# A weight half split inside attention one, banks released one by one, post norms reordered, half-tile stores

## The reference, cut to what matters

```
x = x + conformer_conv(rms_norm(x)); x = x + swiglu(rms_norm(x))       # first block, layer 0
q, k, v, f from rms_norm(x); o = forgetting_attention(q, k, v, f)      # "attention one", 16 heads
x = x + o @ w_o; x = x + moe(rms_norm(x)); x = rms_norm(x)             # layer 1, 8 experts
mix = concat(attention two, gated delta net) @ w_out_2                 # second block
x = x + rms_norm(mix) * post_mix_norm
m = relu(rms_norm(x) @ w_up_2)^2 @ w_down_2
x = x + rms_norm(m) * post_mlp_norm                                    # the output
```

## Time and profile before

| | before |
|---|---|
| time, median of 3 runs | 1800.59 us (1797.88 to 1801.01) |
| the profiled execution | 1803.72 us |
| its span, first to last instruction | 1801.9 us |
| PE busy (matmul) | 1703.9 us, 95% |
| DVE busy | 1272.4 us, 71% |
| ACT busy | 985.6 us, 55% |
| mean granted PE clock | 0.966 of full speed |
| bytes moved | 401.48 MB, mean 223 GB/s |

### The profile page before, as it was taken

One profiled execution on the slowest core, in us unless ns is written; L12 is line 12 of the kernel. 1 busy time (PEld: TensorE's weight loads), 2 busy tenths in 40 slices (PEclk: granted clock), 3 DMA queues, 4 the chain that ended last, 5 costly groups with the idle time before them and its releaser, 6 DMA issues.

```text
span 1801.9 us, 24579 instructions
## 1 busy us (share of the span) xinstructions
PE 1703.9 (95%) x9718; PEld 1493.2 (83%) x9718; DVE 1272.4 (71%) x1306; ACT 985.6 (55%) x1071; POOL 16.2 (1%) x22
## 2 busy tenths in 40 slices
PE   6988999898989999999999999999969999979998
PEld 5867999797878888888888888888859989969997
DVE  4964444545369898888888898988878477555554
ACT  3333444445357777777777776777755441344443
POOL 1000000000000000000000000000000000000000
PEclk9999999899969999999999999999989899989999
DMA  6404554533119898988989898989964300035550
GB/s 267 152 0 187 187 187 164 187 140 141 40 60 373 333 351 323 368 338 347 371 316 369 328 352 331 362 317 372 354 259 164 140 2 1 1 140 187 187 187 24
DMA packets 31189, 401.48 MB, mean 223 GB/s; under 512 B 3688, under 2 KB 3952, under 8 KB 5520
## 3 DMA queue, kind: packets, MB, share of 16 engines
q1 hardware_dynamic: 30704, 399.44, 58.6%
q0 software_dynamic: 416, 1.06, 0.2%
HBM read 399.43 MB, written 1.06 MB: 222 GB/s over the span
## 4 chain that ended last, share of the span: by engine, by line
PE 80%; DVE 8%; DMA 5%; ACT 4%; issue 3%; SPq 0%; DVEq 0%; ACTq 0%
PE ps L1845 21%; PE ps L1847 21%; PE ps L1846 21%; DMA raw<-in_ws 4%; PE ps L1903 3%; DVE wl L876 2%; PE ps L2351 2%; ACT wh L871 2%; PE ps L1919 2%; PE ps L2004 2%; PE ps L2339 1%; PE ps L2161 1%; DMA ring<-in_ws 1%; PE ps L2151 1%; DVE wl L762 1%
## 5 line engine op out<-in xcount | busy, mean ns | idle before, releaser
L876 DVE TENSOR_TENSOR wl<-raw,wh 128x2048 fp32r<-128x2048 f32 x266 | 607.8, 2290 | 90.7 <-ACT wh L871 87.7
L871 ACT ACTIVATE wh<-raw 128x2048 fp32r<-128x2048 f32 x264 | 506.4, 1919 | 200.7 <-PE ps L1847 82.3
L1845 PE MATMUL ps<-wh,f_r 128*128 128x512 f32 (+1 forms) x1200 | 461.3, 384 | 8.9 <-DVE wl L876 6.3
L1846 PE MATMUL ps<-wl,f_r 128*128 128x512 f32 (+1 forms) x1200 | 455.2, 379 | 0.0
L1847 PE MATMUL ps<-wh,f_r 128*128 128x512 f32 (+1 forms) x1136 | 430.3, 379 | 0.0
L1845 PEld LDWEIGHTS ps<-wh,f_r 128*128 128x128 f32 x1200 | 227.0, 189 | 53.7 <-DVE wl L876 9.2
L1846 PEld LDWEIGHTS ps<-wl,f_r 128*128 128x128 f32 x1200 | 227.2, 189 | 40.8
L1845 PE MATMUL ps<-ht_t_r,wh 128*128 128x256 f32 x832 | 241.0, 290 | 8.8 <-DVEq L655 6.6
L1847 PEld LDWEIGHTS ps<-wh,f_r 128*128 128x128 f32 x1136 | 214.3, 189 | 40.4
L1847 PE MATMUL ps<-ht_t_r,wl 128*128 128x256 f32 x832 | 239.8, 288 | 0.0
L1846 PE MATMUL ps<-h_t_r,wh 128*128 128x256 f32 x832 | 238.6, 287 | 0.0
(11 more groups left out here) (406 smaller groups left out, 2017.5 us busy)
## 6 DMA issues: line engine op xcount, KB each, us to landing
raw<-in_ws SPq DMA_DIRECT2D x169, 2048.0 KB, 9.0
raw<-in_ws SPq DMA_DIRECT2D x25, 1024.0 KB, 5.2
ring<-in_ws SPq DMA_DIRECT2D x6, 2048.0 KB, 11.2
gb<-in_gains SPq DMA_DIRECT2D x5, 512.0 KB, 8.5
x_t<-in_x SPq DMA_DIRECT2D x1, 1024.0 KB, 5.0
f<-scratch POOLq DMA_DIRECT2D x8, 128.0 KB, 3.0
out<-x_t SPq DMA_DIRECT2D x2, 512.0 KB, 2.6
cst<-in_const SPq DMA_DIRECT2D x1, 964.5 KB, 6.9
```

The costliest lines, as they stand in the source:

```text
L871: nc.scalar.activation(half_of(wh, h % SPLIT), raw_half(h % HALVES), ACT.Copy).then_inc(S("high"), 1)
L876: nc.vector.tensor_tensor(half_of(wl, h % SPLIT), raw_half(h % HALVES), half_of(wh, h % SPLIT).bitcast(F32), ALU.subtract).then_inc(S("spl ...
L1845: first = nc.tensor.matmul(bank, xh, h, start=start, stop=False)
L1846: nc.tensor.matmul(bank, xh, l, start=False, stop=False)
```

## The change

Four edits. (1) The split of half W2 leaves its place ahead of attention one. ACT makes its high part in two quarters of 1024 columns in steps 4 and 6, DVE the low part in two quarters in steps 8 and 10, each behind that step's exponentials or maxima. (2) DVE frees bank (T,u,j-1) after it has issued the low tiles of bank j (in norm 2: those of the first gain), and only the last one behind the loop. (3) In the post norms DVE adds eps to the first sum of squares in place and multiplies each bank with the norm weights before the root; ACT takes the root of one sum with the other as bias, without the separate addition; behind the root DVE does one multiply-add of M2, the inverse root and X ("mix": one of 1024 columns, "mlp": two of 512). (4) The output goes out in four stores of 256 KB in place of two of 512 KB.

```diff
--- before.py
+++ after.py
@@ -564,9 +564,11 @@
                     sp.wait_ge(S("gb1_used"), 1)
                     sp.dma_start(gb[:, D:2 * D], dr["gains"][3, :].partition_broadcast(P)).then_inc(S("ld_gb1"), 16)
             for tt in range(TT):
-                sp.wait_ge(S("y_ready"), tt + 1)
-                sp.dma_start(out[tt * P:(tt + 1) * P, :], X[:, tt, :]).then_inc(S("stored"), 16)
-            sp.wait_ge(S("stored"), 16 * TT)
+                for c in range(2):
+                    cols = slice(c * 512, (c + 1) * 512)
+                    sp.wait_ge(S("y_ready"), 2 * tt + c + 1)
+                    sp.dma_start(out[tt * P:(tt + 1) * P, cols], X[:, tt, cols]).then_inc(S("stored"), 16)
+            sp.wait_ge(S("stored"), 16 * 2 * TT)
 
 
         @block.gpsimd
@@ -650,9 +652,11 @@
                         src = bank[:, (c % 2) * SEQ:(c % 2 + 1) * SEQ].rearrange("p (t s) -> p t s", t=TT)
                         nc.vector.scalar_tensor_tensor(pair.lo[:, c], src, V(gname, c), pair.hi[:, c].bitcast(F32),
                                                        ALU.mult, ALU.subtract).then_inc(S("ht_lo"), 1)
+                    if j and gname == gains[0][0]:
+                        dve.wait_ge(S("ht_lo"), n - 2 * len(gains))
+                        dve.sem_inc(B.free[B.at[("T", u, j - 1)][0]], 1)
             dve.wait_ge(S("ht_lo"), n)
-            for j in range(4):
-                dve.sem_inc(B.free[B.at[("T", u, j)][0]], 1)
+            dve.sem_inc(B.free[B.at[("T", u, 3)][0]], 1)
 
         def root(dve, ch, tt, order):
 
@@ -725,21 +729,37 @@
                     ins.then_inc(S("q_ready"), 1)
             let_go(B, (name, n), ins)
 
-        def high_pre(act):
-
-            h = count("high_pre")
+        def quarter(a, part):
+            return a[:, part * HALF // 2:(part + 1) * HALF // 2]
+
+        def high_pre(act, quarter_of=None):
+
+            h = todo["high_pre"] if quarter_of == 0 else count("high_pre")
             n, part = pre_unit(h)
             k = (n - N_PRE) % RAW
             act.wait_ge(S(f"ld_w{k}"), 16 * sum(1 for m in range(n + 1) if (m - N_PRE) % RAW == k))
             if h >= SPLIT:
                 act.wait_ge(S("p_used"), h - SPLIT + 1)
-            nc.scalar.activation(half_of(wh, h % SPLIT), half_of(raw, 2 * k + part), ACT.Copy).then_inc(S("p_high"), 1)
-
-        def low_pre(dve):
-
-            h = count("low_pre")
+            if quarter_of is None:
+                nc.scalar.activation(half_of(wh, h % SPLIT), half_of(raw, 2 * k + part), ACT.Copy).then_inc(S("p_high"), 1)
+            else:
+                nc.scalar.activation(quarter(half_of(wh, h % SPLIT), quarter_of), quarter(half_of(raw, 2 * k + part), quarter_of),
+                                     ACT.Copy).then_inc(S("p_high" if quarter_of else "p_quarter"), 1)
+
+        def low_pre(dve, quarter_of=None):
+
+            h = todo["low_pre"] if quarter_of == 0 else count("low_pre")
             n, part = pre_unit(h)
-            dve.wait_ge(S("p_high"), h + 1)
+            if quarter_of == 0:
+                dve.wait_ge(S("p_quarter"), 1)
+            else:
+                dve.wait_ge(S("p_high"), h + 1)
+            if quarter_of is not None:
+                k = 2 * ((n - N_PRE) % RAW) + part
+                nc.vector.tensor_tensor(quarter(half_of(wl, h % SPLIT), quarter_of), quarter(half_of(raw, k), quarter_of),
+                                        quarter(half_of(wh, h % SPLIT), quarter_of).bitcast(F32),
+                                        ALU.subtract).then_inc(S("p_split" if quarter_of else "p_lower"), 1)
+                return
             nc.vector.tensor_tensor(half_of(wl, h % SPLIT), half_of(raw, 2 * ((n - N_PRE) % RAW) + part),
                                     half_of(wh, h % SPLIT).bitcast(F32), ALU.subtract).then_inc(S("p_split"), 1)
 
@@ -820,7 +840,7 @@
                 if s and todo["low_post"] < 2 * N_POST:
                     low_post(dve)
 
-        def attention_act(act, B, a, heads, base):
+        def attention_act(act, B, a, heads, base, beside={}):
 
             PR, PT = PRS[a], PTS[a]
             def heads_out(n):
@@ -845,6 +865,8 @@
                     ins = nc.scalar.activation(PR[:, h % 2, 256:384], bank[:, 256:384], ACT.Exp, bias=rt[:, 65 + m:66 + m],
                                                accum_out=SUMS[:, 0, h:h + 1])
                     let_go(B, ("S", a, h), ins)
+                if h in beside:
+                    beside[h]()
                 if a == 0 and h >= 8 and h % 4 == 0:
                     heads_out((h - 8) // 4)
             if a == 0:
@@ -914,12 +936,10 @@
                     at = tt * D + c * 512
                     nc.scalar.activation(ht_t[:, at:at + 512], bank[:, :], ACT.Square, scale=D ** -0.5,
                                          accum_out=ss[:, 8 + 2 * tt + c:9 + 2 * tt + c]).then_inc(S(name + "_sq"), 1)
-                act.wait_ge(S(name + "_sq"), 3 * tt + 2)
-                nc.scalar.activation(ss[:, 12:13], ss[:, 8 + 2 * tt:9 + 2 * tt], ACT.Identity,
-                                     bias=ss[:, 9 + 2 * tt:10 + 2 * tt]).then_inc(S(name + "_sq"), 1)
-                act.wait_ge(S(name + "_sq"), 3 * tt + 3)
-                nc.scalar.activation(ss[:, 4 + tt:5 + tt], ss[:, 12:13], ACT.Sqrt,
-                                     bias=cst[:, EPSCOL:EPSCOL + 1]).then_inc(S(name + "_root"), 1)
+                act.wait_ge(S(name + "_eps"), tt + 1)
+                act.wait_ge(S(name + "_sq"), 2 * tt + 2)
+                nc.scalar.activation(ss[:, 4 + tt:5 + tt], ss[:, 9 + 2 * tt:10 + 2 * tt], ACT.Sqrt,
+                                     bias=ss[:, 8 + 2 * tt:9 + 2 * tt]).then_inc(S(name + "_root"), 1)
 
         def delta_act(act, ch):
 
@@ -1084,9 +1104,9 @@
             ch(nc.scalar.activation(FA[0:HEADS, 1, :], FA[0:HEADS, 0, :], ACT.Abs))
             ch(nc.scalar.activation(FA[0:HEADS, 1, :], FA[0:HEADS, 1, :], ACT.Exp, scale=-1.0))
             nc.scalar.activation(FA[0:HEADS, 2, :], FA[0:HEADS, 1, :], ACT.Ln, bias=1.0).then_inc(S("f_ln"), 1)
-            for n in range(4):
+            for n in range(3):
                 high_pre(act)
-            attention_act(act, pre, 0, HEADS, 0)
+            attention_act(act, pre, 0, HEADS, 0, {4: lambda: high_pre(act, 0), 6: lambda: high_pre(act, 1)})
             high_pre(act)
 
             norm_act(act, pre, 3, "x_att", 3, [(None, HT)])
@@ -1318,19 +1338,28 @@
 
             dve.wait_ge(S(f"ld_gb{gbn}"), 48 - 16 * gbn)
             for tt in range(TT):
+                for c in range(2):
+                    bank = filled(dve, post, (name, tt, c))
+                    dve.wait_ge(S(name + "_sq"), 2 * tt + c + 1)
+                    if c == 0:
+                        nc.vector.tensor_scalar(ss[:, 8 + 2 * tt:9 + 2 * tt], ss[:, 8 + 2 * tt:9 + 2 * tt], EPS, None,
+                                                ALU.add).then_inc(S(name + "_eps"), 1)
+                    ins = nc.vector.tensor_tensor(M2[:, tt, c * 512:(c + 1) * 512], bank[:, :],
+                                                  gb[:, gbn * D + c * 512:gbn * D + (c + 1) * 512], ALU.mult)
+                    let_go(post, (name, tt, c), ins)
                 dve.wait_ge(S(name + "_root"), tt + 1)
                 ch(nc.vector.reciprocal(ss[:, 6 + tt:7 + tt], ss[:, 4 + tt:5 + tt]))
                 for c in range(2):
-                    bank = filled(dve, post, (name, tt, c))
-                    ins = nc.vector.scalar_tensor_tensor(M2[:, tt, c * 512:(c + 1) * 512], bank[:, :], ss[:, 6 + tt:7 + tt],
-                                                         gb[:, gbn * D + c * 512:gbn * D + (c + 1) * 512], ALU.mult, ALU.mult)
-                    s, k = let_go(post, (name, tt, c), ins)
-                for c in range(2):
                     b, k = post.at[(name, tt, c)]
                     dve.wait_ge(post.free[b], k + 1)
-                    dst = X[:, tt, c * 512:(c + 1) * 512]
-                    ch(nc.vector.tensor_tensor(dst, dst, M2[:, tt, c * 512:(c + 1) * 512], ALU.add))
-                dve.sem_inc(S(done), 1)
+                if name == "mix":
+                    nc.vector.scalar_tensor_tensor(X[:, tt, :], M2[:, tt, :], ss[:, 6 + tt:7 + tt], X[:, tt, :],
+                                                   ALU.mult, ALU.add).then_inc(S(done), 1)
+                else:
+                    for c in range(2):
+                        cols = slice(c * 512, (c + 1) * 512)
+                        nc.vector.scalar_tensor_tensor(X[:, tt, cols], M2[:, tt, cols], ss[:, 6 + tt:7 + tt], X[:, tt, cols],
+                                                       ALU.mult, ALU.add).then_inc(S(done), 1)
 
         def heads(a):
             return a.rearrange("p t (h d) -> p t h d", d=DH)
@@ -1690,10 +1719,11 @@
                     bank = filled(dve, pre, ("v", tt, c))
                     ins = nc.vector.tensor_copy(f2[:, tt * D + c * 512:tt * D + (c + 1) * 512], bank[:, :])
```

(5 more changed lines are left out.)

## The result

The changed kernel takes 1789.59 us, the median of five executions (1785.06 to 1791.67); the kernel before took 1800.59 in the same comparison (five, 1795.73 to 1803.39). The ratio is 0.9939, interval 0.9919 to 0.9959: 11.0 us faster, with an interval of 7.4 to 14.6. Measured a second time, beside the same kernel before, the ratio was 0.995 (0.9938 to 0.9962), 9.0 us. The profiled execution of the changed kernel took 1791.67, with a span of 1789.8; that is 12.1 us less span than before.

A forecast was written before the change was run, and what follows sets the result against it. PE bounds the kernel, with 80% of the chain of waits; the edits target places where the chain leaves it. Terms -4.25 + 0.2 - 1.35 - 1.25 - 0.65 = -7.3 us off 1800.59 gave 1793.3 us, range 1789.8 to 1798.0.

The forecast's parts named there:

- 0.2 lost: Mix post norm, both token tiles: the reordered DVE work finds no idle time to fill and costs 0.2 us more.
- 1.25: Mlp post norm: DVE, idle before, multiplies the first bank while PE works and ends 1.25 us earlier.
- 3.75 + 1.6 - 1.1 = 4.25: Attention one: first transpose 3.75 us earlier, full PE clock behind it 1.6 more, 1.1 lost at step 11.
- The stop at step 11: Attention one: DVE's quarter in step 10 delays the division, so PE stands still 2.0 us instead of 0.86.
- 1610.25: Norm 7: assumed time the second bank is freed, letting PE start at 1610.5, a gain of 1.35 us.
- 0.1 at most: Norm 1: its first product wants the last bank, so freeing banks earlier gains at most 0.1 us.
- rule against small transfers: Output stores: advice to coalesce many small transfers, cited against four stores, whose forecast gain was 0.65 us.
- The clock takes part of it back: Rival, 18%: the longer stop at step 11 brings PE's low clock, a slow stretch costing 1.6 us; 1794.9.
- Attention's end did move with its start: Answers a rival, 8%: ACT and DVE hold attention one's pipeline, edit 1 is worth nothing, 3.05 remain; 1797.5.
- the small edits did show: Answers a rival, 8%: bank release needs the third pair's end and store time is fixed, losing 0.45 and 0.65; 1794.4.
- no step fell to the low clock for long: Answers a rival, 4%: quarters bring attention one to 1.2 GHz, 1.48 us more per step; twelve slow steps make 1811.
- The rule that transposes do not count as PE work: Start of attention one: if it brought the low clock, 1.6 us would be lost, the sum 5.7 instead of 7.3.

The follow-up runs named there:

- quarter in 12: The changed kernel with DVE's second quarter of W2's low part moved from step 10 to step 12, behind the division; 1786.98 us, ratio 0.9923.
- whole stores: The changed kernel with two output stores of 512 KB in place of four of 256 KB; 1789.55 us, ratio 0.9935.
- edit 3 alone: The kernel before with only the post-norm edit, output in two whole-tile stores; 1798.48 us, ratio 0.999.
- changed, again: The changed kernel, unaltered, measured a second time against the kernel before; 1790.15 us, ratio 0.995.
- edit 1 alone: The kernel before with only W2's split moved, in quarters, from ahead of attention one into its steps; 1793.83 us, ratio 0.9965.
- the other form: The changed kernel with the multiplication by the norm weights as a three-operand instruction (bank times 1.0 times weights); 1790.4 us, ratio 0.9941.
- late low: The changed kernel with the scan's last low_post moved from ahead of the mix post norm to behind norm 7's low tiles; 1788.02 us, ratio 0.9934.
- best: The changed kernel with DVE's second quarter in step 12 and the scan's last low_post behind norm 7's low tiles; 1785.38 us, ratio 0.9923.

## Why the forecast was 3.7 too high

Each edit did what the prediction says, and at its place, so the mechanisms stood. The step that failed is the pricing of DVE's work in edit 3: it made "0.2 lost" of a gain of 0.80 in mix and 1.25 of 1.64 in mlp, both outside their bounds, since it priced short operations by their duration and gap (0.2) and every 512-column operation at 0.7, where the runs show 0.06 and, from start to start, 0.60 to 0.67. That is 1.4 of the 3.7. Edit 2's terms for norms 7 and 1 were 0.6 too small together. The last 1.7 stand in no edited place.

- **Edit 1**: forecast 3.75 + 1.6 - 1.1 = 4.25, measured 3.74 (the span from the first score matmul to the first transpose) + 1.61 - 1.14 = 4.2. The stop at step 11 was forecast at 2.0 and is 1.98, and "quarter in 12" shows its cause. The two expert loads went out at 430.67 and 431.29, against 436.09 and 436.71 before, and ACT's quarters were hidden: the idle time ahead of the exponentials of step 5 shrank from 1.21 to 0.27, and none appeared on PE. By that, the cover was nearly used up, and a whole half (1.91) would not have fitted.
- **Edit 2**: forecast 1.35, measured 1.67 in norm 7. The step that was mis-sized is the moment of release: 1610.25 stood in for "between 1610.0 and 1610.9". PE starts 1.82 us into the eight tiles, 0.24 behind the start of the third pair and 0.54 ahead of that of the last. Norm 1 gave 0.28 and not "0.1 at most": the last tile is now followed by one increment where four stood. That this is the cause is argued from the code; no run changes the increments alone. Norms 2 and 5 gave 0, as forecast.
- **Edit 3, mix**: forecast 0.2 lost, measured 0.8 gained; here the sum failed, outside its bounds (0.5 lost, 0.2 gained), and the sign was missed. The order was right (DVE comes late and nothing fills an idle time), the prices were not. I wrote down 0.2 + 1.4 + 0.2 + 1.28 and gaps, 3.15 a tile. By its starts a tile takes 0.06 + 1.20 + 0.23 + 1.20 = 2.69: the eps operation 0.06 and not 0.2, the pair 1.20 and not 1.4, the multiply-add 1.20 and not 1.28. The stop of 0.16 behind the last addition of the kernel before is gone too, since the increment now rides on the operation itself.
- **Edit 3, mlp**: forecast 1.25 with bounds of 0.9 and 1.5, measured 1.64. The second bank's multiplication starts within 0.1 of the forecast; from there to the end I had 5.5, and it took 5.03 (1782.36 to 1787.39), by the same two prices.
- **Edit 4**: forecast 0.65, measured 0.60 by "whole stores"; the other 0.06 of the end column are edit 3's increment. The fixed cost and rate of the Trainium skill ("DMA: Bandwidth & Descriptors", "Anatomy of one DMA") gave 0.6. The Trainium skill states them for DMAs that GpSimd issues; here SP issues, and the trace agrees with the difference: the landing times of 256 and 512 KB lie 0.6 apart. The Trainium skill's rule against small transfers ("DMA: Bandwidth & Descriptors", "Rules for kernel authors"), which the prediction sets against four stores, speaks of those under 64 KB and does not reach these.

Together 4.2 + 1.95 + 0.80 + 1.64 + 0.66 = 9.25 where the forecast had 7.3. That is 2.0 of the 3.7. The bounds had room for it: at their best the terms of the prediction add up to 10.6 (4.57 + 1.6 + 0.2 + 1.8 + 1.5 + 0.9), and not to the 10.2 that it gives. A gain of 9.25 would have been 1791.3, inside the range.

**The other 1.7** stands in no edited place, and what brought it is open. It is not the kernel before's profiled execution, since the forecast was taken off the median. That execution does explain why the two profiled spans lie 12.05 apart: 9.25 in edited places, 2.06 from the levels to the mix product, and 0.74 net elsewhere, by slow stretches that the same kernel has at other places when it runs again. The comparison's interval (7.4 to 14.6) and that of the second measurement (6.8 to 11.2) both hold 9.25, and the second measured 9.0. So the 0.2 us by which the time fell out of the range can be luck. But it is not all luck: of the twelve comparisons ten lie above their local terms, by 1.1 to 3.8 us, and edit 3 alone and "changed, again" lie 0.7 and 0.3 below. The granted clock on record names a candidate. Its mean over the 50 executions of the kernel before is 0.968; for edit 3 alone it is 0.968 too, with no surplus, and for all other kernels 0.970 to 0.974. A mean of 0.001 more is 3.6 us less at 1.2 GHz in a span of 1800, worth up to 1.8 us where PE is busy and nothing where it stands still (an estimate from these figures). So shorter slow stretches are large enough to be the surplus; why edits 1 and 2 would shorten them outside their places, no run shows.

**The rivals.** "The clock takes part of it back" in step 11 (18%) was true of three executions in six: edit 1 alone, the other form and late low had a slow stretch there; changed, changed again and whole stores had none. In the first it cost 1.5, as the rival has it. In the other two the distance from the maxima of step 15 to the addition behind the w_o product was 1.6 shorter than in the others, since that product's own slow stretch was gone: it had only moved. So the rival's mechanism is real in half of the executions, and on average it costs less than the 1.6 that I gave it. Attention's end did move with its start, the small edits did show, and no step fell to the low clock for long. The rule that transposes do not count as PE work (the Trainium skill, "TensorE: Matmul & The Clock Gate", "Part 4: PE-mode transpose") would have brought the low clock at the start; the ten microseconds at 1.00 go against that consequence. They do not test the rule itself, since only 15 of their 70 matmuls are transposes.

## What to carry to other kernels

Split work that stands in front of a pipeline can go into the steps where its engine waits anyway, but look at what is queued behind it there: the same 1.2 us were free in step 12 and cost 1.1 in step 10, where they held up the division that frees PE's bank. Price short vector operations by the distance between starts of such a pair in the trace and not by their durations, and look for instructions with a scalar column that can drop it. Where the clock falls at different places in each execution, take the distances of the edited stages from several traces: here they agree to 0.1 us, while equal kernels were 9.0 and 11.0 us, or 4.5 and 3.4, apart from the one before. And measure the parts of a change alone: the sum of the parts' surpluses shows a gain that no edited place holds, which one comparison of the whole can't tell from luck.

## What the runs showed of the hardware

- DVE takes 747 ns (742 to 751) for 128x512 with a column as the scalar operand, from PSUM (L1325 before) or SBUF (L1361 after), and 680 from PSUM with a constant or none (L1347). Over 1024 columns, with a column, it is 1284.
- An operation of 128x1 costs 0.06 to 0.08 us from start to start when the next waits for nothing, and 0.2 when the next reads its result (0.22 behind the inverse), for the same duration of 0.15.
- PE stood still for 1.98 us at full clock and came back at 1.00 (2.4 GHz) in three executions and was at 0.50 (1.2 GHz) from at most 0.8 us behind the stop in three; after stops of 0.82 (the first transpose, eight executions) and 0.85 (step 11 in quarter in 12 and best) it stayed at 1.00.
- A store of 256 KB moves at about 350 to 440 GB/s (the slices above), little below one of 512 KB. From issue to landing it takes 2.0 us, and one of 512 KB 2.6.
- A slow stretch of PE costs by what PE has to do in it: the one that lay in the mix product of the kernel before cost 1.61 us there, and 0.85 to 0.96 in the kernels that had it in the stage ahead ("to prod.").
